# Layer 1's input projection in one phase, and small inputs read in earlier phases, in a two-layer recurrent backbone

## What is computed

```python
for layer in range(DEPTH):                    # 2
    hl = xl * (1.0 + scale_l) + shift_l
    if layer % 2 == 0:
        pl = hl @ e_w_in[j]
        gl_ = gla_branch(...); rl_ = rwkv_branch(...)
        out_l = jnp.concatenate([gl_, rl_], axis=-1) @ e_w_out[j]
    else:
        pl = hl @ o_w_in[j]
        ml_ = mlstm_branch(...)
        out_l = ml_ @ o_w_out[j]
    xl = layer_norm(alpha * xl + gate_l * out_l, ln_g[layer], ln_b[layer])

def mlstm_branch(...):                        # prep, per grid
    xm, z = split_cols(p, (MLSTM_INNER, MLSTM_INNER))
    xc = jax.nn.silu(depthwise_conv_grid(xm, conv_w, conv_b, grid[0], grid[1]))
    q, k, v = headwise(xc, wq), headwise(xc, wk), headwise(xm, wv)
    # gates: log-sigmoid and input gates of [q, k, v] @ wi, wf, forward and backward
```

## Time and profile before

| | us |
|---|---|
| runs | 3266.6, 3270.16, 3279.11 (median 3270.16) |
| profiled execution | 3269.38, its span 3267.6 |
| TensorE busy | 2596.7 |
| VectorE busy | 1657.3 |
| ScalarE busy | 918.9 |
| GpSimd busy | 849.3 |
| mean granted TensorE clock | 0.89 of 2.4 GHz |

### The profile page before, as it was taken

The page is one execution under the profiler, slowest core; times in us unless marked ns, Lnnn a source line. Parts: engine busy times, 40 slices in busy tenths (PEclk is TensorE's granted clock), DMA queues, the critical chain, the costliest instruction groups (busy, mean ns, idle before and its releaser), DMA issues. The chain is left out here.

```text
span 3267.6 us, 48116 instructions
## 1 busy us (share of the span) xinstructions
PE 2596.7 (79%) x19846; PEld 2212.9 (68%) x19846; DVE 1657.3 (51%) x2457; ACT 918.9 (28%) x1443; POOL 849.3 (26%) x778
## 2 busy tenths in 40 slices
PE   4899999846888753556675989989688989899687
PEld 2577667746777642455564767768588989899575
DVE  2037886533464435887375435435544444444333
ACT  1114323311223214443303222222233333332211
POOL 1211111044655602555222111111011111111322
PEclk8899999977989876778897989999899999999898
DMA  6512554533333213010432233232411212110521
GB/s 249 209 59 82 161 166 136 162 102 80 91 108 77 78 47 81 16 41 33 147 125 62 98 85 100 100 110 71 161 62 72 85 72 85 72 53 1 199 97 58
DMA packets 286368, 317.86 MB, mean 97 GB/s; under 512 B 112083, under 2 KB 233374, under 8 KB 283478
## 3 DMA queue, kind: packets, MB, share of 16 engines
q1 hardware_dynamic: 261152, 314.41, 29.7%
q10 hardware_dynamic: 25014, 0.60, 0.4%
HBM read 202.31 MB, written 112.56 MB: 96 GB/s over the span
## 5 line engine op out<-in xcount | busy, mean ns | idle before, releaser
L2684 PE MATMUL PS<-Q,K 128*128 128x128 f32 x2560 | 302.7, 281 | 62.8 <-DMA Q<-q_d 53.9
L2684 PEld LDWEIGHTS PS<-Q,K 128*128 128x128 f32 x2560 | 298.9, 198 | 65.8 <-DMA Q<-q_d 55.1
L2802 POOL TENSOR_TENSOR weights_lo<-weights,weights_hi 128x1664 fp32r<-128x1664 f32 x32 | 121.4, 3793 | 600.0 <-ACT weights_hi L2760 600.0
L2711 PE MATMUL PS<-V_hi,weights_hi 128*128 128x258 f32 x832 | 238.3, 286 | 5.3 <-DVE H L2910 2.7
L375 PE MATMUL PS<-hT_hi,w_in_hi 128*128 128x512 f32 (+1 forms) x640 | 242.4, 379 | 0.0
L377 PE MATMUL PS<-hT_hi,w_in_lo 128*128 128x512 f32 (+1 forms) x640 | 238.8, 373 | 0.0
L376 PE MATMUL PS<-hT_lo,w_in_hi 128*128 128x512 f32 (+1 forms) x640 | 238.8, 373 | 0.0
L2712 PE MATMUL PS<-V_lo,weights_hi 128*128 128x258 f32 x832 | 235.3, 283 | 0.0
L2713 PE MATMUL PS<-V_hi,weights_lo 128*128 128x258 f32 x832 | 234.5, 282 | 0.0
L375 PE MATMUL PS<-h_hi,w_in_hi 128*128 128x512 f32 (+1 forms) x624 | 228.2, 366 | 5.2 <-PEq L109 5.2
L376 PE MATMUL PS<-h_lo,w_in_hi 128*128 128x512 f32 (+1 forms) x624 | 224.6, 360 | 0.0
(11 more groups left out here) (379 smaller groups left out, 5932.8 us busy)
## 6 DMA issues: line engine op xcount, KB each, us to landing
chunk_in<-in_d SPq DMA_DIRECT2D x40, 512.0 KB, 3.4
w_in<-in_e_w_in_dram SPq DMA_DIRECT2D x30, 512.0 KB, 5.0
xnew<-in_o_w_in_dram SPq DMA_DIRECT2D x30, 512.0 KB, 5.3
in_d<-xnat SPq DMA_DIRECT2D x20, 640.0 KB, 6.2
modw<-in_mod_w_dram SPq DMA_DIRECT2D x8, 1536.0 KB, 19.3
xnat<-in_mod_w_dram SPq DMA_DIRECT2D x8, 1536.0 KB, 7.3
v_d<-xnew SPq DMA_DIRECT2D x16, 640.0 KB, 3.0
k_d<-xc SPq DMA_DIRECT2D x16, 640.0 KB, 2.9
```

What stands on the lines that cost most here:

```text
L2684: last = pe.matmul(PS[:, 4 + x % 4, (j - j0) * P:(j - j0 + 1) * P], K[:, kt, j * P:(j + 1) * P], Q[:, kt, i * P:(i + 1) * P], start=(kt == ...
L2711: pe.matmul(out, wh, VH[:, j, q], start=(j == seen[0]), stop=False)
```

## The change

Four edits. First, `mlstm_inputs` makes all 16 tiles in one phase, without the loop; the clearing of buffers and the load of tile 1's weights move into that phase, behind the first maps on VectorE and at the head of SyncE's list. Second, all of layer 1's maps and columns are read by 16 DMAs (`maps_in`) that layer 0's `out_phase` issues on SyncE's queue at the last k-step of its second group. Third, the attention's constants, gate weights and `lg` are read in `rwkv_units`, between `blocks_out(0)` and `blocks_in(1)`, into buffers that live through both phases; the gate weights' tile is cleared by GpSimd; the bias comes from `G.vc`, whose rows are filled differently in setup. Fourth, in `mlstm_heads` the columns of Q for the first seven query tiles are one DMA, issued when the eighth tile may still be scored, K follows as four DMAs, and Q's last 128 columns as one.

```diff
-                    act.dma_start(rows[V_GBA + 2 * d:V_GBA + 2 * d + 2, 0, :],
-                                  A.p[name][0].rearrange("(i n) -> i n", n=P)).then_inc(s["rows_in"], 16)
+                    act.dma_start(rows[V_GBA:V_GBA + 4, 0, 64 * d:64 * d + 64],
+                                  A.p[name][0].rearrange("(i n) -> i n", n=64)).then_inc(s["rows_in"], 16)
...
+                def gla_in():
+                    sp.dma_start(G.lg[:], A.lg_d).then_inc(s["gla_in"], 16)
+                    for d in range(2):
+                        sp.dma_start(G.wa2[16 * d:16 * d + 16, :, 64 * d:64 * d + 64],
+                                     A.p["gla_wa2_" + "fb"[d]][0].rearrange("r (h c) -> r h c", c=64)).then_inc(s["gla_in"], 16)
+                    sp.dma_start(G.cst0[:], A.consts[:, G.ends[0]:G.ends[1]]).then_inc(s["gla_in"], 16)
...
                 sp.wait_ge(s["zero"], 4)
+                sp.wait_ge(s["wa_zero"], 1)
                 blocks_in(0)
                 blocks_out(0)
+                gla_in()
                 for n in range(HALVES):
...
+                pool.memset(G.wa2[:], 0.0).then_inc(s["wa_zero"], 1)
                 pool.memset(U[:], 0.0).then_inc(s["zero"], 1)
...
-                sp.dma_start(lg[:], A.lg_d).then_inc(s["lr_in"], 16)
-                sp.wait_ge(s["wa_zero"], 1)
-                for d in range(2):
-                    r = slice(64 * d, 64 * d + 64)
-                    sp.dma_start(wa2[16 * d:16 * d + 16, :, r], A.p["gla_wa2_" + "fb"[d]][0].rearrange("r (h c) -> r h c", c=64)).then_inc(s["lr_in"], 16)
-                    for h in range(GLA_HEADS):
-                        sp.dma_start(ba[r, h:h + 1], A.p["gla_ba_" + "fb"[d]][0][64 * h:64 * h + 64].rearrange("(c o) -> c o", o=1)).then_inc(s["lr_in"], 16)
-                sp.dma_start(G.cst0[:], A.consts[:, G.ends[0]:G.ends[1]]).then_inc(s["cst_in"], 16)
...
                         if late(g, k - 2) is not None:
                             finish(late(g, k - 2))
+                        if extra and g == 1 and k == n_k - 1:
+                            n_extra = extra(sp, s["extra_in"])
...
-        with phase(nc, "zero w_in") as (block, s):
+        with phase(nc, sems) as (block, s):
+            w_in, stored = [s["w_in0"], s["w_in1"]], [s["stored0"], s["stored1"]]
+
             @block.sync
             def _(sp):
-                load_w(sp, 0, 1, s["w_in"])
-                sp.wait_ge(s["w_in"], 32)
+                load_w(sp, 1, w_in[1])
+                for t in range(TILES):
+                    if t + 2 < TILES:
+                        if t:
+                            sp.wait_ge(s["hi_ok"], t)
+                            sp.wait_ge(s["lo_ok"], t)
+                        load_w(sp, t + 2, w_in[t % 2])
...
+                maps(0)
                 dve.memset(B.gates[:], 0.0)
-                dve.memset(padl[:].rearrange("p a b -> p (a b)"), 0.0)
+                dve.memset(WG[:], 0.0)
                 dve.memset(padc[:], 0.0)
-                dve.memset(WG[:], 0.0).then_inc(s["zero"], 1)
+                dve.memset(padl[:].rearrange("p a b -> p (a b)"), 0.0).then_inc(s["zero"], 1)
+                dve.wait_ge(s["zero"], 1)
+                folds(0)
...
-        with nc.Fori(0, HEADS1 - 1) as r:
-            head_round(r, True)
-        head_round(HEADS1 - 1, False)
...
+                def load_q(h):
+                    sp.dma_start(Q[:, :, 0:last], B.q_d[h * 4:h * 4 + 4, :, 0:last].rearrange("k p t -> p k t")).then_inc(s["q_in"], 16)
+
+                def load_q_last(h):
+                    sp.dma_start(Q[:, :, last:], B.q_d[h * 4:h * 4 + 4, :, last:].rearrange("k p t -> p k t")).then_inc(s["q_last_in"], 16)
...
                         sp.wait_ge(s["d_ok"], TQ * (h + 1))
                         load_rows(h + 1)
+                        sp.wait_ge(s["scored"], 3 * (TQ * h + TQ - 1))
+                        load_q(h + 1)
+                        sp.wait_ge(s["skip_ok"], 4 * (h + 1))
                         sp.wait_ge(s["scored"], 3 * TQ * (h + 1))
-                        sp.wait_ge(s["skip_ok"], 4 * (h + 1))
-                        load_qk(h + 1)
+                        load_k(h + 1)
+                        load_q_last(h + 1)
...
+            def maps_in(eng, sem):
+                eng.dma_start(B.cols[:], A.cols1_d.rearrange("i p j -> p i j")).then_inc(sem, 16)
+                for j, n in enumerate(("ml_wq", "ml_wk", "ml_wv")):
+                    eng.dma_start(B.wqkv[:, :, j], A.p[n][0].rearrange("j c d -> (j c) d").rearrange("(t p) d -> p t d", p=P)).then_inc(sem, 16)
+                for j, n in enumerate(("ml_wi_f", "ml_wf_f", "ml_wi_b", "ml_wf_b")):
+                    for a in range(3):
+                        eng.dma_start(B.wg[:, :, a, j], A.p[n][0][a * INNER:(a + 1) * INNER].rearrange("(t p) h -> p t h", p=P)).then_inc(sem, 16)
+                return 16
```

More of the change, by code:

```diff
@@ L1097, in _ @@
                 sp.wait_ge(s["st"], 64)
+                sp.wait_ge(s["gla_in"], 64)
             @block.tensor
@@ L2063, with out_phase @@
 YRING = 3
-def out_phase(nc, A, G, layer, yT_d, w_out, n_k, tiles, x_of, xnew, store):
+def out_phase(nc, A, G, layer, yT_d, w_out, n_k, tiles, x_of, xnew, store, extra=None):
     with ExitStack() as ctx:
@@ L2147, in _ @@
                     sp.wait_ge(stored[i], 16 * (len(tiles) // 2))
+                if extra:
+                    sp.wait_ge(s["extra_in"], 16 * n_extra)
             @block.tensor
@@ L2336, in _, with maps, folds @@
+            @block.gpsimd
+            def _(pool):
+                for t in range(1, TILES):
+                    pool.wait_ge(s["hi_ok"], t)
+                    if t >= 2:
+                        pool.wait_ge(s["z_ps"], t - 1)
+                        pool.wait_ge(s["lo_ok"], t - 1)
+                    low_part(pool, t % 2).then_inc(s["lo_ok"], 1)
             @block.vector
             def _(dve):
+                step = Steps(dve, s["step"])
+                def maps(t):
+                    if t >= 2:
+                        dve.wait_ge(s["v_ps"], 3 * (t - 1))
+                    for j in range(3):
+                        last = dve.tensor_tensor(BD[:, t % 2, j].rearrange("p (a b) -> p a b", b=4), wqkv[:, t, j:j + 1, :].broadcast_to([P, 32, 4]),
+                                                 G.c("block4").rearrange("p (a b) -> p a b", b=4), ALU.mult)
+                    last.then_inc(s["bd_ok"], 1)
+                def folds(t):
+                    dve.wait_ge(s["fold_ps"], t + 1)
+                    if t >= 2:
+                        dve.wait_ge(s["gate_ps"], t - 1)
+                    dve.tensor_copy(WG[:, t % 2, :, 0:16], PS[:, 7, 0:32].rearrange("p (j n) -> p j n", j=2)).then_inc(s["fold_sb"], 1)
+                    dve.tensor_copy(BQK[:, t % 2], PS[:, 7, P:2 * P]).then_inc(s["bqk_sb"], 1)
+                maps(0)
@@ L2600, in mlstm_heads @@
         sems = ("zero rows_in rows_in2 bias_in x_ok l_ok rows_ok gturned cols_ok m_st pcol_in floor_ok gstep gact_step "
-                "row_in qk_in v_in skip_in v_hi v_lo w_hi w_lo scored weighted d_ok diag_ok av_ps av_sb mean_ok root normed "
+                "row_in k_in q_in q_last_in v_in skip_in v_hi v_lo w_hi w_lo scored weighted d_ok diag_ok av_ps av_sb mean_ok root normed "
                 "turned skip_ok y_half y_ok step stored")
@@ L3027, in build @@
         B.gates = sb("gates1", [P, LRT])
-        with nc.sbuf_tensor("cst_rwkv", [P, G.ends[2] - G.ends[1]], F32) as G.cst_rwkv:
+        with ExitStack() as early:
+            G.cst_rwkv = early.enter_context(nc.sbuf_tensor("cst_rwkv", [P, G.ends[2] - G.ends[1]], F32))
             with nc.sbuf_tensor("LW", [P, T], F32) as LW, nc.sbuf_tensor("LA", [P, T], F32) as LA:
@@ L3033, in build @@
                         project_phase(nc, A, G, xnat, hi, lo, LW, LA)
+            G.cst0 = early.enter_context(nc.sbuf_tensor("cst0_gla", [P, G.ends[1] - G.ends[0]], F32))
+            G.wa2 = early.enter_context(nc.sbuf_tensor("wa2", [32, GLA_HEADS, P], F32))
+            G.lg = early.enter_context(nc.sbuf_tensor("lg", [32, T], F32))
             rwkv_units(nc, A, G)
-        gla_units(nc, A, G)
+            gla_units(nc, A, G)
         with ExitStack() as c1:
+            B.cols, B.wqkv, B.wg = (c1.enter_context(nc.sbuf_tensor(n, [P, NT1] + x, F32))
+                                    for n, x in (("tile_cols", [TILE_PARAMS]), ("wqkv", [3, 4]), ("w_gates", [3, 4, 4])))
+            def maps_in(eng, sem):
[6 more added lines that the diff above has]
+                return 16
             xnew = c1.enter_context(nc.sbuf_tensor("xnew", [P, NCH, D], F32))
```

396 lines of the change are left out of this document (169 added, 227 removed).

## The result

Four executions of the changed kernel take 3215.5 to 3221.8 us, median 3218.8; four of the kernel before 3266.6 to 3279.1, median 3273.9. The medians lie 55 us apart, the ratio is 0.984 [0.983, 0.985], which is 53 us less; the forecast was 59 less. The profiled execution took 3219.4 us, its span is 3217.6.

The account below looks back on a forecast made before the run. TensorE, busy 2597 of 3268 us, was taken as the bound, so its holes are what can be won. 51.6 + 6.7 + 6.5 - 8 + 1.9 = 58.7 us off 3269.4 gives 3211 us, range 3201 to 3236.

Parts of the forecast that it names:

- Part 1: Layer 1's inputs: one phase of 16 tiles removes three joints, saving 51.6 us; the clearing phase goes, saving 6.7.
- Part 2: Attention's constants and small inputs read in the recurrent phase: 8.9 us saved, 2.4 lost, net 6.5 us.
- The start's gain: Attention's start: TensorE's first matmul no longer waits for constants, 8.9 us saved.
- The loop's price: Recurrent phase's serial loop of SyncE and GpSimd: issuing four early DMAs costs 2.4 us, bounds 0 to 5.
- Part 3: Layer 0's output projection: 20.6 us of maps on SyncE's queue ahead of y loads delay the last group 8 us.
- The delay neither grows nor shrinks: Output projection's last group: VectorE's norms pace it at 6.3 us each as before, so the 8 us delay stays.
- Part 4: Between layer 1's heads: next queries still stand behind the eighth tile's decay; less Q awaited saves 1.9 us in all.
- some 8 each, if the early load did run: Between heads: upper bound of Part 4, nearly the whole wait saved at each of three boundaries.
- Maps slow: Output projection: maps take longer to generate than move, 45 or 57 us; delay 33 to 44, 3236 to 3247; chance 0.12.
- slower than before: Output projection: 2 KB stride makes map pieces so dear the last group starves, from 79 us of maps; chance 0.03.
- the early queries: Between heads: the queries do come early, saving 3 x 8 us rather than 1.9, giving 3189 us; chance 0.05.
- the longer period: Layer 1's inputs: the long phase runs at a tile period of 35 us, giving back 36 us, 3247; chance 0.04.

Follow-up runs that it names:

- part 2 alone: Kernel before, with only the attention's constants and small inputs read in the recurrent phase: 3269.3 us, ratio 0.9985.
- part 1 alone: Kernel before, with only layer 1's inputs as one phase of 16 tiles, clearing phase gone, maps issued in modulate_split's phase: 3218.2 us, ratio 0.983.

## Why the prediction was right, and where it was off

The forecast was 3211 us, the range 3201 to 3236; measured 3218.8. It started from the profiled execution of 3269.4; from the median of the kernel before, 3273.9, the same 58.7 us lead to 3215, and the medians give 55. By landmarks, from the pair of profiles 50.5 us apart:

**Part 1** was right in both terms, 51.6 against 51.4 and 6.7 against 6.8, and alone in its own kernel too. The bound on a longer period (7 us) wasn't needed.

**Part 2.** The start's gain was right, 8.9 against 9.1. The loop's price was undersized: 2.4 us forecast, the issue alone; 3.9 in the changed kernel's phase. The first period grew by 3.4 there and by 4.1 in the mean of eight profiles (61.9 against 57.8 in the five without loads in the loop), since the load of the constants slows the blocks' trip. The prediction had this as its upper bound of 5 and had no row for it. Net it gave part 2 6.5 us; alone it measured 5.2 [1.6, 8.2]. That the loop has no slack holds in the mean of the profiles (3.6 us more in the whole stretch).

**Part 3.** The size and the mechanism were right: 21.6 us of maps against 20.6, a wait of ScalarE named by y's DMA, TensorE idle 13.8 us (forecast some 15), the last root 8.1 late against 8. But the 8.1 are made up otherwise. The delay at root 4 was 6.2, not 8, because the maps' issue began 0.5 us behind that of x, where the prediction let them start 4 us behind it, with x landed; that outweighs 1.0 us more of maps and 4.2 us for landing and copies where 3.5 were put down. "The delay neither grows nor shrinks" failed: the norms behind it came 6.46 and 6.47 us apart rather than 6.27 and 6.28, and a stretch at a lower granted clock added 1.6, with maps or without. That the last root is late by 8.1, as forecast, is therefore in part luck.

**Part 4.** Right: the early load stands behind `d_ok`, the queries go with M_row, the wait stays at 7 to 9 us; 1.9 forecast, 2.7 in the changed kernel, 0.1 alone, which three rounds can't tell apart. The bound "some 8 each, if the early load did run" was too low: set free together with K, it gives 28 us. All of the wait goes (23.8 us in the mean), and a wait also costs the clock behind it.

**What the sum left out** are the 5.8 us of the attention and 2.5 us ahead of the first store of blocks, 8.3 together: the whole difference between 58.7 and 50.5. The prediction had put nothing there, as no edit touches either. The start is 684.4 to 689.2 us over fourteen profiles, of which 684.4 is part 2 alone with the changed setup; an effect of the bias rows is not shown, and 2.5 us is within this spread. The loop's price, 1.5 us above its forecast, and the 0.7 us won ahead of the first `q_out` with the 0.8 more in the heads nearly cancel.

Of the rivals, none came. "Maps slow" and "slower than before" fell with 0.66 ns per piece, the early queries with their issue 0.37 us behind M_row, and the longer period with 32.07 us. The figure of about 10.5 ns per packet in the Trainium skill, "DMA: Bandwidth & Descriptors", section "Bandwidth", is that of a small load issued from GpSimd. It isn't borne out as a price in one stream on SyncE's queue: 344 us would have been the time, 21.6 were measured.

## What to carry to other kernels

A load that is moved earlier is free only if nothing on its queue is awaited behind it: ask for each place what stands next on that list, and who paces it. The same edit (maps) cost 6 us in one phase and nothing in the next. And a wait put before an "early" load makes it late: the order on the list decides, not the load's own wait. When one experiment gains more than its edit can, compare the landmarks of stretches that it doesn't touch before giving it the difference of two medians. The largest gain of this change, 58 us, is the removal of three joints in a pipeline; by the medians the changed kernel with all four parts is no faster than part 1 alone (3218.8 against 3218.2).

## What was not expected of the hardware

- A wait of 7.3 to 8.9 us on TensorE is followed by 3.7 to 5.2 us at a granted clock of 0.50, about 2 us more lost (estimated from the spans).
- The same instructions of the attention take 327.5 to 333.6 us in kernels with the same code in that phase. The difference comes in steps of 1.0 to 1.8 us, each in a stretch of lower granted clock; one kernel gave 333.6 in both of its profiles.
- A load of 1.1 MB on the same queue just ahead of small dependent round trips lengthens such a trip from 10.2 us to 10.9 to 13.0.
- Of the maps' DMAs of 2048 pieces, the last 13 hold SyncE 1.1 to 1.3 us each (the attention's 1088 KB of constants took 0.58), and each lands some 4 us after its issue began: what stands behind them on the list is late before its own data moves.
